# Turning retention's normed values with VectorE and sixteen transfers instead of TensorE, in a one-core hybrid encoder layer

## What is computed

```python
def head_rms(y):
    yf = y.astype(jnp.float32)
    return (yf * lax.rsqrt(jnp.mean(yf * yf, axis=-1, keepdims=True) + EPS)).astype(y.dtype)

# retention, last lines: y is (B, S, 4 heads, 128), g is the gate from the input projection
    y = (inner + cross).reshape(B, S, H, dv)
    y = head_rms(y) * jax.nn.silu(g)
    return y.reshape(B, S, H * dv)

# hybrid_mixer: each branch output goes through its own matrix and gate
    ys = jnp.stack([y_a, y_b, y_c], axis=2)
    yb = jnp.einsum('bsnc,ncd->bsnd', ys, w_branch)
    g = jax.nn.sigmoid(gates.reshape(B, S, N_BRANCH, D_MODEL))
    return jnp.sum(g * yb, axis=2) @ w_out
```

## Time and profile before

| what | us |
|---|---|
| time before, median of 3 runs (lowest to highest) | 948.47 (948.39 to 948.69) |
| the profiled execution, its own time | 948.88 |
| its span, first to last instruction | 947.1 |
| TensorE busy | 934.4 |
| VectorE busy | 614.9 |
| ScalarE busy | 416.6 |

### The profile page before, as it was taken

How to read it: one execution, slowest core, us unless ns; L and a number is a source line. 1 busy time by engine, 2 the same in 40 slices (tenths; PEclk the granted TensorE clock), 3 DMA queues, 4 the chain that set the end, 5 groups by cost and what they waited for, 6 DMA issues and landing times.

```text
span 947.1 us, 11739 instructions
## 1 busy us (share of the span) xinstructions
PE 934.4 (99%) x4524; PEld 774.4 (82%) x4524; DVE 614.9 (65%) x728; ACT 416.6 (44%) x472; POOL 100.7 (11%) x116
## 2 busy tenths in 40 slices
PE   7999999999999999999999999999999999999997
PEld 6878888777888888888888887888888888888886
DVE  5877555454679554466545557777777677777776
ACT  6463213331763562233334355534333343454664
POOL 1024242200242000000021003100000000000002
PEclk9999999999999999999999999999999999999999
DMA  7458797122678643323423213343334333254553
GB/s 251 169 155 240 194 247 197 45 79 67 155 198 203 179 112 100 99 68 111 134 89 107 93 45 111 89 133 89 89 90 114 107 89 89 89 198 179 186 190 125
DMA packets 133892, 125.53 MB, mean 133 GB/s; under 512 B 5626, under 2 KB 113502, under 8 KB 133726
## 3 DMA queue, kind: packets, MB, share of 16 engines
q1 hardware_dynamic: 123854, 101.66, 34.6%
q0 software_dynamic: 9856, 23.07, 11.0%
q10 hardware_dynamic: 144, 0.26, 0.1%
HBM read 122.88 MB, written 25.17 MB: 156 GB/s over the span
## 4 chain that ended last, share of the span: by engine, by line
PE 93%; DVE 4%; ACT 2%; DMA 0%; issue 0%; SPq 0%; DVEq 0%; ACTq 0%
PE ps L598 69%; PE ps L1107 6%; PE ps L1119 5%; PE ps L972 5%; PE ps L652 1%; PE ps L752 1%; PE ps L743 1%; PE ps L736 1%; PE ps L986 1%; PE ps L1002 1%; DVE wL L1548 1%; PE ps L758 1%; DVE hgF L1548 0%; DVE hgG L1740 0%; DMA invf<-in_consts 0%; ACT L1167 0%
## 5 line engine op out<-in xcount | busy, mean ns | idle before, releaser
L598 PE MATMUL ps<-hH,wH 128*128 128x512 f32 x784 | 308.3, 393 | 2.5 <-DVE wL L1548 2.1
L598 PE MATMUL ps<-hH,wL 128*128 128x512 f32 x784 | 305.3, 389 | 0.0
L598 PE MATMUL ps<-hL,wH 128*128 128x512 f32 x784 | 305.1, 389 | 0.0
L1548 DVE TENSOR_TENSOR wL<-raw,wH 128x2048 fp32r<-128x2048 f32 (+3 forms) x119 | 209.4, 1767 | 59.5 <-ACT wH L1167 59.2
L1167 ACT ACTIVATE wH<-raw 128x2048 fp32r<-128x2048 f32 (+3 forms) x119 | 176.0, 1488 | 145.6 <-PE ps L598 145.0
L598 PEld LDWEIGHTS ps<-hH,wH 128*128 128x128 f32 x784 | 147.2, 188 | 35.7 <-DVE wL L1548 3.5
L598 PEld LDWEIGHTS ps<-hH,wL 128*128 128x128 f32 x784 | 147.1, 188 | 30.9
L598 PEld LDWEIGHTS ps<-hL,wH 128*128 128x128 f32 x784 | 147.2, 188 | 30.2 <-issue 0.2
L1167 ACT ACTIVATE ca<-za,par 128x512 f32<-128x512 f32 x22 | 17.9, 816 | 97.5 <-DVE za L1548 97.5
L1555 DVE SCALAR_TENSOR_TENSOR ca<-za,par,ca 128x512 f32<-128x512 f32 x44 | 33.1, 751 | 26.9 <-ACT ca L1167 24.1
L1555 DVE SCALAR_TENSOR_TENSOR cu<-zu,par,cu 128x512 f32<-128x512 f32 x44 | 33.1, 752 | 26.8 <-ACT cu L1167 24.0
(11 more groups left out here) (301 smaller groups left out, 1469.4 us busy)
## 6 DMA issues: line engine op xcount, KB each, us to landing
raw<-in_w_in SPq DMA_DIRECT2D x57, 512.0 KB, 4.5
raw<-in_w_up SPq DMA_DIRECT2D x44, 512.0 KB, 4.5
t<-in_w_down POOLq DMA_DIRECT2D x66, 256.0 KB, 5.4
raw<-t SPq DMA_DIRECT2D x11, 768.0 KB, 4.7
raw<-in_w_branch SPq DMA_DIRECT2D x24, 256.0 KB, 4.3
t<-t POOLq DMA_DIRECT2D x22, 256.0 KB, 9.3
raw<-in_w_down SPq DMA_DIRECT2D x10, 512.0 KB, 4.3
raw<-in_w_out SPq DMA_DIRECT2D x8, 512.0 KB, 4.0
```

What stands on the lines that cost most here:

```text
L598: last = pe.matmul(out_ap, a, b, start=start and k + m == 0, stop=stop and m == 2 and k == len(terms) - 1)
L1548: q.sig(dve.tensor_tensor(out_ap, a, b, op), sem)
```

## The change

TensorE's sixteen transposes go. VectorE, right after it has normed `rYt`, turns it in four instructions, one for each 128 rows, in blocks of 32x32, into `rblk`. Sixteen transfers of 64 KB from SBUF to SBUF put the blocks in place (`rT`): eight are issued by SyncE between its loads of slots 21 and 22, after a wait for all four turns (`r_turn`), and eight between the loads of slots 22 and 23. The product with the gate moves from job 20 to the head of job 21, reads `rT` from SBUF in four instructions instead of one, and waits for all sixteen transfers (`r_in`); `yaH` moves with it. `yaL` moves from job 21 to the end of slot 23. TensorE's `s_scores(0)` no longer waits for `r_yf`.

```diff
+        rblk = at("rblk", U[2], [P, 4, H, NT, 32])
+        rT = at("rT", U[4], [P, 4, H, NT, 32])
...
                 load_gate(Slot(c), 2 if c < N_G1 else 0, (c - N_G0) % KD)
+                if c in (21, 22):
+                    sp.wait_ge(r_turn, NT)
+                    for m in range(8 * (c - 21), 8 * (c - 20)):
+                        a, k = m // 4, m % 4
+                        sp.dma_start(rT[32 * k:32 * k + 32, a], rblk[32 * a:32 * a + 32, k]).then_inc(r_in, 16)
                 if c == N_G0 + 8:
...
-                elif n == 19:
-                    pe.wait_ge(r_yt, 1)
+                elif n == 20:
                     pe.wait_ge(sv_ready, 1)
-                    for h in range(H):
-                        transposes([(ps[:, 4 + h, P * i:P * i + P], rYt[:, i, P * h:P * h + P]) for i in range(NT)],
-                                   r_T)
-                elif n == 20:
-                    pe.wait_ge(r_yf, 1)
                     pe.wait_ge(s_rope, 3)
                     pe.wait_ge(s_kd, 1)
                     s_scores(0)
...
-                elif n == 20:
-                    act.wait_ge(r_yf, 1)
-                    do(yaH[:, :, :], rY[:, :, :], ACT.Copy, r_hi)
                 elif n in (21, 22):
+                    if n == 21:
+                        act.wait_ge(r_yf, 1)
+                        do(yaH[:, :, :], rY[:, :, :], ACT.Copy, r_hi)
...
-                    tt(y, y, statr[:, :].unsqueeze(2).to_broadcast([P, 16, P]), ALU.mult, r_yt)
-                elif n == 20:
+                    tt(y, y, statr[:, :].unsqueeze(2).to_broadcast([P, 16, P]), ALU.mult)
+                    q.settle()
+                    for t in range(NT):
+                        q.sig(dve.transpose(rblk[:, :, :, t, :].rearrange("p c h i -> p h c i"),
+                                            rYt[:, t, :].rearrange("p (h c j) -> p h c j", c=4, j=32)), r_turn)
+                elif n == 21:
                     dve.wait_ge(r_g, 1)
-                    dve.wait_ge(r_T, H)
-                    tt(rY[:, :, :], rG[:, :, :], ps[:, 4:8, :], ALU.mult, r_yf)
-                elif n == 21:
+                    dve.wait_ge(r_in, 16 * 16)
+                    for h in range(H):
+                        y, g = (u[:, h, :].rearrange("p (t a i) -> p t a i", a=4, i=32) for u in (rY, rG))
+                        tt(y, g, rT[:, :, h].rearrange("p a t i -> p t a i"), ALU.mult, r_yf if h == H - 1 else None)
+                    q.settle()
                     softmax_in(0)
-                    dve.wait_ge(r_hi, 1)
-                    tt(yaL[:, :, :], rY[:, :, :], yaH[:, :, :].bitcast(F32), ALU.subtract, ya_ready)
...
                     gate_out(n, mix[:, c - N_G0, :])
+                    if c == 23:
+                        dve.wait_ge(r_hi, 1)
+                        tt(yaL[:, :, :], rY[:, :, :], yaH[:, :, :].bitcast(F32), ALU.subtract, ya_ready)
```

More of the change, by code:

```diff
@@ L349, in hybrid_layer @@
              "lev_out lev_kq lev_taken hg_o hg_sq hg_sum hg_ms hg_std hg_rs hg_row hg_yf hg_hi yc_ready")
-        (r_sw, r_rope, r_sc, r_att, r_g, r_o, r_sqd, r_ms, r_std, r_yt, r_T, r_yf, r_hi, ya_ready) = sems(
-            "r_sw r_rope r_sc r_att r_g r_o r_sqd r_ms r_std r_yt r_T r_yf r_hi ya_ready")
+        (r_sw, r_rope, r_sc, r_att, r_g, r_o, r_sqd, r_ms, r_std, r_turn, r_in, r_yf, r_hi, ya_ready) = sems(
+            "r_sw r_rope r_sc r_att r_g r_o r_sqd r_ms r_std r_turn r_in r_yf r_hi ya_ready")
         sv_T, sv_ready = sems("sv_T sv_ready")
```

## The result

The changed kernel takes 961.13 us (median, 960.41 to 962.31), the kernel before beside it 948.43: ratio 1.0131, interval 1.0118 to 1.0143, so 12.7 us slower by the medians and 12.4 by the ratio. The forecast was 956.1 in a range of 951.5 to 961.5. The sign and the mechanism held; the size came out 5 us too small, and the time lies only 0.4 us inside the upper end of the range.

What follows compares the result with a forecast made beforehand. TensorE's line was taken as the bound, the softmax path nearly a second; load(22), queued late, delays job 22 by 7.6 us with the 1.67 saving lost inside: 948.88 + 7.6 = 956.5, less 0.4 for the median, 956.1, range 951.5 to 961.5.

Steps and rivals of the forecast that it cites:

- Which bounds: TensorE's line bounds, its transposes worth 1.67 us; the softmax path is nearly a second bound, 0.35 us slack before job 22.
- rival 3: SyncE's queue is not the cause, load(22) lands in time: 949.0 us, +0.5; chance 0.05 no change, 0.02 faster.
- The turns: Four turns of 128x512 on VectorE in job 19: 2.48 us, up to 5.0 if two passes; r_turn complete about 273.4.
- The issues on SyncE's queue: Eight transfers ahead of load(22) at 0.43 us each: 3.5 us, range 3.0 to 4.6; load(22) out at 276.9.
- The landing of load(22): Load(22), issued beside GpSimd's round, lands 9.4 us after its second issue, at 286.7; range 4.9 to 10.7 us.
- From the landing to the first `sP`: wH(22), wL(22), rY in four instructions, then softmax_in(0): together 10.57 us, first sP ready at 297.3.
- TensorE's two waits: TensorE waits about 7 us at s_scores(1) in job 21, another 2.2 before job 22, which starts 7.6 us later.
- The second eight transfers: Issued behind load(22), 277.9 to 281.4, needed by rY at 289.9: just in time at 8.2 us, +2.2 at 10.7.
- What follows: After slot 23, later yaL, memtok and load(26): 0 to 2.9 us possible, taken as 0, so +7.6 us stays.
- rival 1: Same mechanism, larger stall, from binding transfers, two-pass turns, slow issues, slow landing or late load(26): 958 to 961.5 us, chance 0.27.
- the prediction's reading of the earlier trace against that rule: On the DMA engines, queues do not look to take equal turns by packet, since q1 stood still beside a full q0.

Runs made afterwards that it cites:

- run 4: The kernel before without TensorE's sixteen transposes, nothing added, the product reading unturned values: 946.76 us, ratio 0.9979.
- 3: The changed kernel without the sixteen transfers and SyncE's wait; turns and four-instruction product stay ahead of softmax_in(0): 949.10 us, ratio 1.0010.
- 9: The changed kernel with the first eight transfers reading HBM instead of SBUF, same size and shape: 961.46 us, ratio 1.0139.
- 5: The changed kernel with GpSimd's rounds from the tenth on held back by six slots: 954.88 us, ratio 1.0062.
- 7: The changed kernel without the second eight transfers, the product using and waiting for the first eight only: 960.60 us, ratio 1.0129.
- 2: The changed kernel without the sixteen transfers, SyncE's wait for the turns kept ahead of load(22): 950.33 us, ratio 1.0018.
- 8: The changed kernel with four transfers of 256 KB instead of sixteen of 64 KB, two ahead of load(22): 953.45 us, ratio 1.0041.
- 12: The changed kernel with eight transfers behind load(22) and eight behind load(23), the product still ahead of softmax_in(0): 960.47 us, ratio 1.0126.

## Why the prediction was right, and where it was short

- **Which bounds.** Right. The transposes are worth 1.8 us by the medians and 2.0 by the ratio (run 4), for 1.67 expected, and the softmax path is a second bound with 0.35 us of slack: 3 gave +0.6 to 0.9 where the working of rival 3 had +0.5. The step 18.0 from one `sP` to the next came out 18.0.
- **The turns.** 2.48 taken, 2.49 measured; `r_turn` complete at 272.73, forecast 273.4 less the 0.65. The Trainium skill (Vector Engine (DVE) Microarchitecture Reference, The reshape front-end and per-opcode configuration) says the transposing mode sustains one element a cycle and lane; the trace agrees, as a turn took what a plain operation of 128x512 takes.
- **The issues on SyncE's queue.** This term failed by size. Eight at 0.43 were to take 3.5 us (upper bound 4.6); they took 6.10, 0.76 each on average. It cost +2.6 us. The row I took was of 128-partition loads from HBM; no row showed a 32-partition transfer or one from SBUF. The usual one of the eight took 0.59, and eight of 0.59 with the 0.04 us between two issues make 5.0; the rest of 1.1 is one long issue and one pause, which 9 shows to come with transfers from HBM too. From the chain of work after the change (start, us, what):

```profile
273.40 0.59 SPq L497
274.00 0.04 issue
274.04 1.32 SPq L497
275.36 0.04 issue
275.40 0.59 SPq L497
275.99 0.44 issue
```

- **The landing of load(22).** Second failure by size: 9.4 taken, range 4.9 to 10.7, measured 11.3, +1.9 us. The mechanism, that GpSimd's round holds the DMA engines, is shown by 5: 5.5 us without it. I had the two rows of loads beside a round, 10.6 and 10.7, and took less than either for no reason that the rows gave.
- **From the landing to the first `sP`.** 10.57 forecast, 10.65 measured.
- **TensorE's two waits.** About 7 and 2.2 us were forecast; the first was 11.94, the second never came, because TensorE ran at a lower clock after the first. The prediction took 15.73 us from the one job to the other; at that clock they were some 17.8 (an estimate, worked out in the last section). The sum came through by luck, because the path's 18.0 was just longer.
- **The second eight transfers.** Taken as just in time; 7 shows that they add nothing.
- **What follows.** Load(26) came late, by 2.50 us for ScalarE, and 1.28 us of idle time before `sPT` were left: covered, as taken.
- **Rivals.** What happened is rival 1, the same mechanism with a larger stall, 958 to 961.5: slow issues (+2.6) and slow landing (+1.9) on top of +7.6, in sum 12.1 of the measured 12.5; the rest is mostly load(22)'s own second issue, 0.63 us after its first instead of 0.41, and 0.08 in the path. The other side (rival 3) would have needed load(22) to land 2.3 us after issue.
- **The range.** It held by luck. Both terms that failed lie beyond their stated bounds (6.1 us of issues for 4.6 at most, 11.3 of landing for 10.7 at most), and the two upper bounds together would have given 958.5. The range reached to 961.5 because rival 1 also allowed for transfers that bind, turns of two passes and a late load(26), and none of these cost anything.

The loss by runs (ratios, in us of 948.5): -2.0 for the transposes, then +2.9 (3) for the turns and the product in the path, +0.8 (2) for the wait, +4.2 (5) for transfers and issues with no round beside them, +6.5 for GpSimd's round, 12.4 in sum (12.7 by the medians). The +0.8 for the wait is within the intervals of 2 and 3, and their profiles show the same waits of TensorE, so it is not shown to be above nothing. This is one order of taking them away; the table shows that the parts do not add, so another order would share them out differently.

## What to carry to other kernels

A transfer put on a queue costs what stands behind it: price its issues, the wait ahead of them, and where the next load then falls among other engines' transfers, not only its own bytes. Where two waits lie in parallel, removing one shows the other at nearly the same length; run the two removals together before calling either harmless. Price an issue by a row of the same shape and source, add the pause between two, and leave room for a long one; where the rows beside a known collision agree, take them. And look at the single issues before reading a cause out of their mean: in 9 the mean did not move and the usual issue did.

## What the runs showed that was not expected

- An issue on SyncE took 0.76 us on average for 64 KB on 32 partitions, 0.73 from HBM, and 0.71 in a row of sixteen, with a median of 0.59 (0.42 from HBM) and single ones of up to 4.13 us. A 512 KB load took 0.37, and 0.58 behind the transfers. The Trainium skill (DMA: Bandwidth & Descriptors, Anatomy of one DMA — SWDGE (gpsimd) path) gives the sequencer's dispatch of a transfer as some 50 ns, for GpSimd's path; SyncE's own time for the usual one from SBUF is over ten times that, and it is what the load queued behind.
- GpSimd's queue gets far more than half of the DMA engines. After the change, in the window 282:285, while load(22) waits:

```profile
q0 software_dynamic: 239, 0.44, 88.0%
q1 hardware_dynamic: 180, 0.15, 19.3%
```

- With the rounds held back, in 281:284, SyncE's queue moves nearly six times as much:

```profile
q1 hardware_dynamic: 1393, 0.86, 104.7%
```

  In packets the first window is 239 to 180, not far from the turns by packet that the Trainium skill (DMA: Bandwidth & Descriptors, Queues, rings and completion order) describes; in time it is 88 to 19, since a packet of q0 is larger (1.8 KB for 0.8) and takes over three times as long. The kernel before has a window with the turns in full, 273:274, while load(22) was under way there too:

```profile
q0 software_dynamic: 92, 0.16, 88.8%
q1 hardware_dynamic: 91, 0.05, 22.3%
```

  So the prediction's reading of the earlier trace rows against that rule rested on one window. In 269:270, less than 2 us behind the issue of the load, q1 has no packet; in 271:272 the counts are 101 to 5, in 273:274 92 to 91. Whether q1 had anything ready in the first of these no view shows. The rule can hold and the load still land late; that it holds throughout is not shown.
- In the wait of 11.94 us TensorE's clock fell. Its last product before the wait starts at 289.24, the pieces of job 21 at 301.56. The windows of 2 us of the changed kernel (TensorE's share first, the granted clock in the third column from the right) show 0.50, its lower level of 1.2 GHz, from 294 to 306, and 0.99 in the next one; the kernel before has 1.00 from 280 to 320.

```profile
294.00:296.00 2.00, 0.00 (x0) 0.00 (x0) 2.00 (x5) 0.00 (x0) 2.00 (x4) 0.50 0.49 92
304.00:306.00 2.00, 2.00 (x16) 1.68 (x13) 0.40 (x1) 1.99 (x3) 0.33 (x1) 0.50 0.08 16
306.00:308.00 2.00, 2.00 (x10) 1.64 (x9) 1.38 (x2) 0.87 (x1) 1.32 (x2) 0.99 0.46 51
```

  The 32 pieces of job 21 took 3.79 us instead of 2.06, and the first products behind them ran at the lower clock too. This used up the second wait: TensorE's last product ahead of job 22 starts at 319.12, and by the 0.23 us between two products it could have begun job 22 at about 319.35 (an estimate), 0.15 before the second `sP`. A little more, and the clock would have set the time. It did so in 5, 8 and 12: there job 22 begins 18.26, 18.31 and 18.42 us after job 21's pieces begin, 0.3 to 0.5 us after the second `sP` is ready.
